# A hybrid attention and state-space block: the recurrence in rounds of two pairs of groups

## What is computed

```python
z = rms_norm(x, norm_mix) @ w_in
q, k, v, u, g = jnp.split(z, splits, axis=-1)
bu = einsum(u, B)                           # per group: 16 channels -> 64 complex states
h  = associative_scan(h[t] = A * h[t-1] + bu[t])
y  = Re(C h) + D u                          # 32 groups
branch_b = (gelu(y) * sigmoid(gelu(y) @ w_glu + b_glu)) @ w_ssm_branch
g_a, g_b = split(sigmoid(g))
x = x + (g_a * branch_a + g_b * branch_b) @ w_out
```

## Time and profile before

| | |
|---|---|
| median of 3 runs (lowest, highest) | 2452.63 us (2452.57, 2452.85) |
| profiled execution, first to last instruction | 2449.8 us |
| what lies around that span, by the median | 2.8 us |
| PE busy | 2406.2 us, 98% of the span |
| PE's weight loads busy | 1972.8 us, 81% |
| DVE, ACT, POOL busy | 1728.3, 747.6, 849.4 us |
| recurrence, slots 0 to 17, block 0 | from 247.85 us |
| the same, block 1 | from 1453.71 us |

### The profile page before, as it was taken

The page is one execution under the profiler, slowest core; times in us unless marked ns, Lnnn a source line. Parts: engine busy times, 40 slices in busy tenths (PEclk is TensorE's granted clock), DMA queues, the critical chain, the costliest instruction groups (busy, mean ns, idle before and its releaser), DMA issues.

```text
span 2449.8 us, 33368 instructions
## 1 busy us (share of the span) xinstructions
PE 2406.2 (98%) x11578; PEld 1972.8 (81%) x11578; DVE 1728.3 (71%) x2569; ACT 747.6 (31%) x1431; POOL 849.4 (35%) x689
## 2 busy tenths in 40 slices
PE   7999999999999999999999999999999999999997
PEld 6887778887788888878888877788878888888886
DVE  6964555646899999989750346455478888888896
ACT  4145114212333333332222441142233333333222
POOL 2421223440555555523232222235114333333221
PEclk9999999999999999999999999999999999999999
DMA  6266553441344334598522636535212222217963
GB/s 208 75 179 129 169 170 125 154 174 69 106 143 146 133 124 151 205 367 296 184 94 86 125 101 194 153 121 184 117 52 95 86 77 77 91 64 266 344 227 137
DMA packets 178279, 367.35 MB, mean 150 GB/s; under 512 B 22344, under 2 KB 60008, under 8 KB 178168
## 3 DMA queue, kind: packets, MB, share of 16 engines
q1 hardware_dynamic: 135568, 278.23, 34.9%
q10 hardware_dynamic: 42600, 87.64, 10.4%
HBM read 277.20 MB, written 88.60 MB: 149 GB/s over the span
## 4 chain that ended last, share of the span: by engine, by line
PE 93%; DVE 3%; DMA 2%; ACT 1%; issue 1%; SPq 0%; POOL 0%; DVEq 0%; POOLq 0%; ACTq 0%
PE ps L497 29%; PE ps L499 29%; PE ps L498 29%; PE ps L2240 1%; PE ps L2242 1%; PE ps L2222 1%; PE ps L2190 1%; PE ps L2179 1%; PE ps L2041 1%; DMA ff<-z 1%; PE ps L2091 0%; DVE act_lo L1852 0%; PE ps L2170 0%; DMA step_w<-tw 0%; PE ps L2168 0%
## 5 line engine op out<-in xcount | busy, mean ns | idle before, releaser
L844 POOL CAST slot_hi<-pair_raw 128x512 fp32r<-128x512 f32 x220 | 201.7, 924 | 394.8 <-PE ps L499 310.0
L497 PE MATMUL ps<-act_hi,w_hi 128*128 128x512 f32 x832 | 330.9, 398 | 0.0
L499 PE MATMUL ps<-act_hi,w_lo 128*128 128x512 f32 x832 | 324.6, 390 | 0.0
L498 PE MATMUL ps<-act_lo,w_hi 128*128 128x512 f32 x832 | 323.8, 389 | 0.0
L798 POOL CAST w_hi<-w_raw 128x1024 fp32r<-128x1024 f32 x72 | 77.3, 1074 | 657.9 <-PE ps L499 648.5
L497 PE MATMUL ps<-act_hi,slot_hi 128*128 128x512 f32 x704 | 274.3, 390 | 1.8 <-DVE pre L1805 1.5
L499 PE MATMUL ps<-act_hi,slot_lo 128*128 128x512 f32 x704 | 273.9, 389 | 0.0
L498 PE MATMUL ps<-act_lo,slot_hi 128*128 128x512 f32 x704 | 273.9, 389 | 0.0
L497 PE MATMUL ps<-act_hi 128*128 128x512 f32 x616 | 241.4, 392 | 5.3 <-DVE act_lo L1856 5.3
L498 PE MATMUL ps<-act_lo,act_hi 128*128 128x512 f32 x616 | 240.4, 390 | 0.0
L499 PE MATMUL ps<-act_hi,act_lo 128*128 128x512 f32 x616 | 240.3, 390 | 0.0
(11 more groups left out here) (324 smaller groups left out, 4932.3 us busy)
## 6 DMA issues: line engine op xcount, KB each, us to landing
w_raw<-in_wu SPq DMA_DIRECT2D x88, 512.0 KB, 3.6
pair_raw<-in_wu SPq DMA_DIRECT2D x88, 512.0 KB, 4.1
step_f<-ff SPq DMA_DIRECT2D x88, 512.0 KB, 5.2
ff<-z SPq DMA_DIRECT2D x44, 512.0 KB, 2.6
gates<-junk ACTq DMA_DIRECT2D x64, 256.0 KB, 2.1
sig<-gates ACTq DMA_DIRECT2D x32, 512.0 KB, 5.3
tbl_o<-tables ACTq DMA_DIRECT2D x32, 384.0 KB, 3.6
step_w<-in_wu SPq DMA_DIRECT2D x22, 512.0 KB, 6.0
```

The lines of the kernel that those rows point to most:

```text
L497: nc.tensor.matmul(out, lh, rh, start=first, stop=False, skip_group_check=onto)
L498: nc.tensor.matmul(out, lh, rl, start=False, stop=False, skip_group_check=onto)
L499: return nc.tensor.matmul(out, ll, rh, start=False, stop=last, skip_group_check=onto)
L844: nc.gpsimd.tensor_copy(slot_hi[j][:, :, :], src).then_inc(slot_half[KIND[j]], 1)
```

## The change

PE's 18 slots become nine rounds, n = 0, 2, ... 16. A round is: the state inputs of pairs n and n+1, the outputs of states of pairs n-2 and n-1, the outputs of inputs of pairs n-2 and n-1, and the gate halves 12+n and 13+n. ACT's loop is put in the same order: both y outputs of a round, then both gate halves. No instruction is added or taken away; DVE, POOL and SP have the same code as before.

```diff
-                for n in range(PAIRS + 2):
-                    if n >= 2:
-                        m = n - 2
+                for n in range(0, PAIRS + 2, 2):
+                    for m in range(n - 2, n) if n >= 2 else ():
                         act.wait_ge(y_done, blk * PAIRS + m + 1)
...
                     gate_out(12 + n)
+                    gate_out(13 + n)
                     if n in (8, 12, 16):
                         y_high(n // 4 - 2)
...
+                def of_states(m):
+                    b, tab = m % 3, tbl_o[m % NO]
+                    pe.wait_ge(h_ready, blk * PAIRS + m + 1)
...
+                for n in range(0, PAIRS + 2, 2):
                     if n < PAIRS:
...
+                        state_in(n)
+                        state_in(n + 1)
                     if n >= 2:
...
+                        of_states(n - 2)
+                        of_states(n - 1)
+                        of_inputs(n - 2)
+                        of_inputs(n - 1)
                     gate(12 + n)
+                    gate(13 + n)
                 gate(GATES - 2)
                 gate(GATES - 1)
```

More of the change, by code:

```diff
@@ L2213, in _ @@
                 pe.wait_ge(steps_in, 16 * STEP * (blk + 1))
-                for n in range(PAIRS + 2):
-                    if n < PAIRS:
[L2216 to L2225, removed]
-                    if n >= 2:
[L2227 to L2243, removed]
@@ new lines, in state_in @@
+                def state_in(m):
+                    pe.wait_ge(rec_in[m % NR], table_count(blk, m, NR))
+                    if m >= 2:
+                        pe.wait_ge(sin_read, blk * PAIRS + m - 1)
+                    for ri in range(2):
+                        for g in range(2):
+                            ins = mm(ps[SS * g:SS * g + SS, s_bank[m % 2], ri * P:(ri + 1) * P],
+                                     tbl_r[m % NR][:, TB_W + ri * P + SS * g:TB_W + ri * P + SS * g + SS], ssT[:, 2 * m + g, :],
+                                     start=True, stop=True)
+                    ins.then_inc(sin_done, 1)
@@ new lines, in of_states @@
+                def of_states(m):
+                    b, tab = m % 3, tbl_o[m % NO]
+                    pe.wait_ge(h_ready, blk * PAIRS + m + 1)
+                    if m >= 2:
+                        pe.wait_ge(y_evac, blk * PAIRS + m - 1)
+                    pe.wait_ge(outp_in[m % NO], table_count(blk, m, NO))
+                    if m == 0:
+                        pe.wait_ge(attn_ready, (blk + 1) * TT)
+                    for ri in range(2):
+                        for g in range(2):
+                            rows, c = slice(SS * g, SS * g + SS), TB_V - TB_T + 256 * ri + P * g
+                            mm(ps[:, y_bank[m % 2] + g, 0:P], tab[rows, c:c + P], s_h[b][rows, ri, 0:NCH], start=ri == 0, stop=False)
@@ new lines, in of_inputs @@
+                def of_inputs(m):
+                    for g in range(2):
+                        ins = mm(ps[:, y_bank[m % 2] + g, 0:P], tbl_o[m % NO][:, g * P:(g + 1) * P], ssT[:, 2 * m + g, :],
+                                 start=False, stop=True)
+                    ins.then_inc(y_done, 1)
+                for n in range(0, PAIRS + 2, 2):
+                    if n < PAIRS:
+                        state_in(n)
+                        state_in(n + 1)
+                    if n >= 2:
+                        of_states(n - 2)
+                        of_states(n - 1)
+                        of_inputs(n - 2)
+                        of_inputs(n - 1)
```

## The result

| | before | after |
|---|---|---|
| median of 5 runs each, side by side | 2452.63 us | 2531.82 us |
| ratio, with its 95% interval | | 1.0323 (1.0312 to 1.0335) |
| span of the profiled execution | 2449.8 us | 2528.8 us |

The change made the kernel slower by 79.2 us. The forecast was 2534 us, with a range from 2500 to 2557.

A forecast was written before the change was run, and what follows sets the result against it. PE, busy 98% of the span, was taken to bound the kernel. Stops less savings (+57.0 us) and clock loss (+24.2 us) made +81 us on 2452.6, so 2534 us, range 2500 to 2557.

The forecast's parts named there:

- What PE saves: PE's small matmul groups: a second group of one form back to back pays its passes alone, 9.8 us saved in all.
- What PE waits for: Output of states of pair n-1 needs DVE's states; the wait existed before, its cover of 5.43 us of gate is gone.
- The stop: PE idle before the second output of states in each of 14 full rounds, 4.8 us each.
- DVE's answer: From the state input's start to DVE's last write of the states: 6.10 us with POOL's subtraction, 3.96 as lower bound.
- From DVE to PE: Handover from DVE's last write of the states to PE's next matmul: 0.14 us.
- The round: Length of a full round on PE with its stop: 18.91 us against 14.72 for two slots, +57.0 us net in all.
- The clock: TensorE's clock falls to half after each of 14 stops, losing 1.73 us each time, +24.2 us in all.
- The sum: Whole kernel: 57.0 + 24.2 = +81 us, giving 2534 us; chance 0.58.
- POOL out of DVE's way: Rival: POOL's subtraction falls elsewhere, each round 2.1 us shorter; 2480 us, or 2504 with the clock; chance 0.08.
- The stop without the clock: Rival: PE stops as forecast but TensorE's clock stays up; 2510 us; chance 0.2.
- A longer low clock: Rival: half clock holds twice as long after each stop; 2557 us; chance 0.1.
- The gain alone: Rival: states of pair n-1 are ready before the round, PE runs through and gains 9.8 us; 2443 us; chance 0.04.

The follow-up runs named there:

- the run with stops of 2.27 us: The change with the gate halves moved on by one (12 before round 0, then 13+n and 14+n in each round): 2492.14 us, ratio 1.0162.

## Why the prediction was right

Step by step, as the prediction put them:

- **What PE saves**, 9.8 us: measured 9.7 (2452.63 to 2442.89), or 10.3 against the runs of the kernel before beside it (2453.16). A round without stops was to take 14.14 us and took 14.12.
- **What PE waits for.** The order on DVE told which wait would lose its cover. All 14 stops are there, and they go when DVE's order is turned round or a gate half put between. One step is worded wrongly: before, the state input stood one slot ahead of the output that needs it, 7.36 + 0.59 = 7.95 us by the earlier trace rows, not one slot and a gate half. The slot holds the one gate half that was the cover, so nothing hung on it.
- **The stop**, 4.8 us, of which the profile was to show 4.6 to 4.9: it shows 4.4. By the starts of the matmuls PE stands still for 4.7 us (286.79, less 280.64 + 1.02 + 0.44); the profile counts from the modelled end of the matmul before (0.71 us behind its first start, not 0.44), and the prediction did not take that off.
- **DVE's answer**, 6.10 us: the states end 6.04 to 6.10 us after the round's start, and in every round POOL's subtraction is in it, as it was in the even slots from 2 to 14 before.
- **From DVE to PE**, 0.14 us: this term was too large. It is 0.05 us in the round shown. The row that it came from was PE's wait for a longer DVE operation at another place.
- **The round**, 18.91 us at full clock: 20.34 measured (from 260.45 to 382.46, six rounds), less 1.6 for the clock, 18.75. The 0.16 too much is mostly the handover (0.09), and 0.03 in the outputs of inputs.
- **The clock**, 1.73 us a stop: 1.6 by the timeline and 1.5 by the filled stop. It fell at each of the 14. The choice to take it for all 14 rested on one row, of a longer stop, and came out; the run with stops of 2.27 us shows that the length of a stop does not decide it alone.
- **The sum**, 81 us: measured 79.2, and the forecast is 2.2 us too high. Some of that closeness is luck. A round was put at 18.91 + 1.73 = 20.64 us and took 20.34, and 14 times the 0.30 too much is 4.2 us. By the trace the 14 rounds grew by 5.62 us each, less some 1.6 for rounds 0 and 16: 77 us. The spans differ by 79.0, so some 2 us came from outside the recurrence, 0.5 of them ahead of its first round (248.33 against 247.85), where both kernels have the same code. No step of the prediction had these 2 us.
- **What costs nothing.** ACT waits longer for its stores than before and nobody waits for ACT.

Of the rivals, "POOL out of DVE's way" is the run with the gates moved on, which came out between its 2480 and 2504. "The stop without the clock" was put at 2510; with the clock kept up by the filled stop the kernel took 2508.23. "A longer low clock" did not show behind stops of 4.4 us; of the falls at the stops of 2.27 us two of six were that long. "The gain alone" was put at 2443, with the condition that the scan of pair n-1 does not stand behind the state input of pair n; with that condition made true the kernel took 2442.89.

## What to carry to other kernels

When work is grouped to save a fixed cost, look for the waits whose cover was the work between the groups, and read in the order of the *other* engine's queue what its answer stands behind; here a wait for the next input in front of the finishing of the last one turned a saving of 10 us into a loss of 79. The remedy was on the engine that was waited for: let it finish what it has before it waits for new input, and the grouping pays. A stop of a few us costs more than its length when the clock falls behind it. Where such a stop has to stay, it can pay to fill it with matmuls that are thrown away: here 18 of them in each of 14 stops took the kernel from 2531.82 to 2508.23 us.

## What the runs showed of the hardware

- The granted clock fell to 0.50 at all 14 stops of 4.4 us, each time for 3.4 us, and at 6 of 14 stops of 2.3 us, all of one length. A stop of 1.51 us in the feed-forward part left it at 1.00.
- A copy of 128 x 2 elements on VectorE took 0.16 us alone and 2.30 us beside GpSimd's subtraction of two SBUF tiles, ending with it (284.39 and 284.36).
- Between matmuls with 64 rows and matmuls with 128 rows and columns the change of form cost TensorE about 0.2 us (two more in a round, one each way, 0.39 us).
